# Gate rows of the expert layer: one wide comparison on VectorE, three gated rows on GpSimd, two plain rows on ScalarE

## The reference, cut to what matters

```python
s1 = jnp.einsum('thd,kd->thk', q[..., :half], sub_keys[0])
s2 = jnp.einsum('thd,kd->thk', q[..., half:], sub_keys[1])
v1, i1 = lax.top_k(s1, PEER_TOPK)
v2, i2 = lax.top_k(s2, PEER_TOPK)
top, pos = lax.top_k(cand, PEER_TOPK)      # cand: v1 + v2, all 16 x 16 pairs
eidx = jnp.take_along_axis(cidx, pos, axis=-1)   # i1 * 128 + i2
gate = jax.nn.softmax(top, axis=-1)
act = jax.nn.gelu(jnp.einsum('td,thkd->thk', hc, expert_u[ec]))
return jnp.einsum('thk,thkd->td', gate * act, expert_v[ec])
```

## Time and profile before

| | |
|---|---|
| median of 3 runs | 3121.25 us (3119.77 to 3121.68) |
| the profiled execution | 3119.68 us, its span 3117.9 us |
| TensorE busy | 2938.2 us (94%) |
| VectorE busy | 1988.4 us (64%) |
| ScalarE busy | 1313.5 us (42%) |
| GpSimd busy | 270.8 us (9%) |
| mean granted TensorE clock | 0.97 |

### The profile page before, as it was taken

How to read it: one execution, slowest core, us unless ns; L and a number is a source line. 1 busy time by engine, 2 the same in 40 slices (tenths; PEclk the granted TensorE clock), 3 DMA queues, 4 the chain that set the end, 5 groups by cost and what they waited for, 6 DMA issues and landing times.

```text
span 3117.9 us, 48959 instructions
## 1 busy us (share of the span) xinstructions
PE 2938.2 (94%) x17330; PEld 2555.8 (82%) x17330; DVE 1988.4 (64%) x3635; ACT 1313.5 (42%) x2096; POOL 270.8 (9%) x387
## 2 busy tenths in 40 slices
PE   8897899999999987988999999998999898999898
PEld 5674799999999864877999999997977887978797
DVE  4669866777767634797666666665556654555664
ACT  1235844444444412575444444444443433534333
POOL 0026600000000000473000000000000000000000
PEclk9898999999999997999999999999999998999899
DMA  8532166666666641303555665664334454424354
GB/s 329 193 114 81 42 189 222 226 232 229 223 233 231 204 156 71 143 8 108 189 187 186 195 191 191 194 193 164 128 132 166 152 186 150 151 108 163 141 176 148
DMA packets 130807, 524.30 MB, mean 168 GB/s; under 512 B 17981, under 2 KB 28093, under 8 KB 108025
## 3 DMA queue, kind: packets, MB, share of 16 engines
q1 hardware_dynamic: 120648, 508.13, 47.6%
q10 hardware_dynamic: 10034, 14.52, 1.4%
HBM read 519.44 MB, written 3.16 MB: 168 GB/s over the span
## 4 chain that ended last, share of the span: by engine, by line
PE 76%; issue 8%; DVE 6%; ACT 6%; DMA 1%; DVEq 1%; ACTq 1%; PEld 0%; POOL 0%; SPq 0%; PEldq 0%; POOLq 0%
PE prob_ps L1247 22%; PE acc L1259 22%; PE acc L927 7%; PE acc L912 3%; PE acc L1474 3%; PE acc L886 3%; PE acc L1489 3%; PE acc L865 3%; PE acc L1424 2%; ACT arena L1810 2%; PE turn_ps L1020 2%; PE acc L1449 1%; PE acc L994 1%; ACT arena L1800 1%; PE turn_ps L940 1%
## 5 line engine op out<-in xcount | busy, mean ns | idle before, releaser
L1247 PEld LDWEIGHTS prob_ps<-hTr,utr 128*128 128x128 f32 x5856 | 734.5, 191 | 26.5 <-issue 8.6
L1247 PE MATMUL prob_ps<-hTr,utr 128*128 128x256 f32 x5856 | 745.4, 284 | 2.3 <-issue 1.2
L1259 PE MATMUL acc<-vr,wtr 128*128 128x512 f32 x2964 | 718.8, 391 | 1.1 <-DVE vr L2550 1.1
L1259 PEld LDWEIGHTS acc<-vr,wtr 128*128 128x128 f32 x2964 | 541.0, 188 | 103.9 <-issue 1.7
L2550 DVE TENSOR_TENSOR vr<-slab,vr 128x1024 fp32r<-128x1024 f32 x246 | 301.4, 1225 | 408.3 <-ACT vr L1848 408.3
L1848 ACT CAST vr<-slab 128x1024 fp32r<-128x1024 f32 x246 | 258.2, 1050 | 577.8 <-PE acc L1259 570.0
L2525 DVE TENSOR_TENSOR utr<-slab,utr 128x1024 fp32r<-128x1024 f32 x244 | 297.3, 1218 | 11.9 <-ACT utr L1821 11.9
L1821 ACT CAST utr<-slab 128x1024 fp32r<-128x1024 f32 x244 | 255.4, 1047 | 8.2 <-issue 4.8
L2104 POOL TENSOR_TENSOR small<-small 128x2 f32<-128x2 f32 (+3 forms) x18 | 20.8, 1155 | 2695.5 <-DVE small L2176 1458.0
L2807 DVE TENSOR_TENSOR slab_lo<-slab,w_hi 128x2048 fp32r<-128x2048 f32 x64 | 143.8, 2288 | 124.1 <-ACT w_hi L2076 124.1
L2076 ACT CAST w_hi<-slab 128x2048 fp32r<-128x2048 f32 x64 | 119.2, 1906 | 159.2 <-DMA slab<-in_pack_b 150.7
(11 more groups left out here) (292 smaller groups left out, 4137.6 us busy)
## 6 DMA issues: line engine op xcount, KB each, us to landing
slab<-in_pack_b SPq DMA_DIRECT2D x132, 1024.0 KB, 4.9
slab<-in_peer_v SPq DMA_DIRECT2D x255, 512.0 KB, 3.5
slab<-in_peer_u SPq DMA_DIRECT2D x244, 512.0 KB, 4.6
arena<-in_pack_a SPq DMA_DIRECT2D x84, 512.0 KB, 4.7
slab<-in_pack_a SPq DMA_DIRECT2D x40, 1024.0 KB, 7.1
arena<-in_peer_u SPq DMA_DIRECT2D x6, 1024.0 KB, 14.2
slab<-in_pack_b SPq DMA_DIRECT2D x4, 832.0 KB, 5.4
arena<-in_pack_a SPq DMA_DIRECT2D x2, 1024.0 KB, 18.6
```

Source lines behind the costliest of these rows:

```text
L1247: ins = pe.matmul(prob_ps[:, m % 2, 0:S], utr[:, m % 2, uh, k * P:k * P + P], hTr[:, hh, k, :], start=(k == 0 and n == 0), stop=(k == KD - ...
L1259: ins = pe.matmul(y_ps[:, t, n, :], wtr[:, m % 2, wh, t * P:t * P + P], v[:, vh, n * 512:n * 512 + 512], start=first and k == 0, stop=last ...
```

## The change

GpSimd makes the first three gated rows (POOLQ = 3) in place of four plain ones; a gated row compares and multiplies in one instruction and reads two values for each partition. ScalarE makes the first two plain rows (ACTQ = 2) in place of three in the middle. VectorE makes the other six plain rows by one instruction, a comparison of two tiles (128 x 768, `iota` repeated over the rows against the keys repeated along the columns), and then the five gated rows 3 to 7. The number of instructions in a group goes from 9 to 6 on VectorE, from 4 to 3 on GpSimd and from 5 to 4 on ScalarE, counting its copy. GpSimd additionally waits at the start of a layer for the copy of the gates, "pairs1", and two semaphores get other names.

```diff
-POOLQ = 4
+POOLQ = 3
-ACTQ = 3
+ACTQ = 2
...
-                    at = n * TOKG + POOLQ
+                    at = n * TOKG
                     for q in range(ACTQ):
                         act.activation(key_gap[:, q], iota[:], ACT.Square, bias=pairsT[:, 1, at + q:at + q + 1], scale=-1.0)
                     act.drain()
-                    act.activation(rows[:, n % 2, 1, POOLQ:POOLQ + ACTQ, :], key_gap, ACT.Relu, bias=1.0, scale=-1.0)\
+                    act.activation(rows[:, n % 2, 1, 0:ACTQ, :], key_gap, ACT.Relu, bias=1.0, scale=-1.0)\
                         .then_inc(act_rows.sem, 1)
...
-                nc.gpsimd.wait_ge(*turns.emptied_at("a", l, "pairs0"))
-                nc.gpsimd.sem_inc(passed["pool"], 1)
+                for use in ("pairs0", "pairs1"):
+                    nc.gpsimd.wait_ge(*turns.emptied_at("a", l, use))
+                    nc.gpsimd.sem_inc(passed["pool"], 1)
                 for n in range(S // TOKG):
...
-                        ins = nc.gpsimd.tensor_scalar(rows[:, n % 2, 1, q, :], iota[:], pairsT[:, 1, tok:tok + 1],
-                                                      None, ALU.is_equal)
-                    ins.then_inc(plain_rows.sem, 1)
+                        ins = nc.gpsimd.tensor_scalar(rows[:, n % 2, 0, q, :], iota[:], pairsT[:, 0, tok:tok + 1],
+                                                      pairsT[:, 2, tok:tok + 1], ALU.is_equal, ALU.mult)
+                    ins.then_inc(pool_rows.sem, 1)
...
                 for n in range(S // TOKG):
                     dve.wait_ge(*gates_full.two_before("a", l, n + 1))
-                    for q in range(TOKG):
+                    at = n * TOKG + ACTQ
+                    dve.tensor_tensor(rows[:, n % 2, 1, ACTQ:TOKG, :], spread(iota[:], 1, TOKG - ACTQ),
+                                      spread(pairsT[:, 1, at:at + TOKG - ACTQ], 2, P), ALU.is_equal)
+                    for q in range(POOLQ, TOKG):
                         tok = n * TOKG + q
-                        dve.tensor_scalar(rows[:, n % 2, 0, q, :], iota[:], pairsT[:, 0, tok:tok + 1],
-                                          pairsT[:, 2, tok:tok + 1], ALU.is_equal, ALU.mult)
-                    for q in range(POOLQ + ACTQ, TOKG):
-                        tok = n * TOKG + q
-                        ins = dve.tensor_scalar(rows[:, n % 2, 1, q, :], iota[:], pairsT[:, 1, tok:tok + 1], None,
-                                                ALU.is_equal)
-                    ins.then_inc(gated_rows.sem, 1)
+                        ins = dve.tensor_scalar(rows[:, n % 2, 0, q, :], iota[:], pairsT[:, 0, tok:tok + 1],
+                                                pairsT[:, 2, tok:tok + 1], ALU.is_equal, ALU.mult)
+                    ins.then_inc(dve_rows.sem, 1)
```

More of the change, by code:

```diff
@@ L286, in two_blocks @@
         pairs_ready = Signal(sem("pairs_ready"), a=2)
-        gated_rows = Signal(sem("gated_rows"), a=S // TOKG)
-        plain_rows = Signal(sem("plain_rows"), a=S // TOKG)
+        dve_rows = Signal(sem("dve_rows"), a=S // TOKG)
+        pool_rows = Signal(sem("pool_rows"), a=S // TOKG)
         act_rows = Signal(sem("act_rows"), a=S // TOKG)
@@ L1225, in _ @@
                 for n in range(S // TOKG):
-                    pe.wait_ge(*gated_rows.at("a", l, n + 1))
-                    pe.wait_ge(*plain_rows.at("a", l, n + 1))
+                    pe.wait_ge(*dve_rows.at("a", l, n + 1))
+                    pe.wait_ge(*pool_rows.at("a", l, n + 1))
                     pe.wait_ge(*act_rows.at("a", l, n + 1))
```

## The result

The changed kernel takes 3171.93 us (median of 4 runs, 3166.99 to 3174.36) against 3121.47 (4 runs). The ratio is 1.016, with a 95% interval of 1.0142 to 1.0178: slower by 1.6%, some 50 us. The forecast was 3124.2 with a range of 3110 to 3142, so the result lies 30 us above its upper end. The profiled execution took 3171.95, its span 3170.2.

What follows compares the result with a forecast made beforehand. ScalarE's chain was taken to bound the gates stage at 2.561 us a group; afterwards a loop of 2.60: 59 x (2.60 - 2.561) = +2.3, start +0.6, together +2.9 us, median 3124.2 us, range 3110 to 3142.

Steps and rivals of the forecast that it cites:

- ScalarE's load: Gates stage, kernel before: ScalarE's chain sets the period of 2.561 us a group; after the change its load is 2.17.
- the stage's time is carried to the end one to one: Expert loop behind the gates stage: TensorE busy 523.85 of 524 us, so the stage's gain or loss isn't hidden there.
- VectorE's wide comparison: Gates stage, VectorE: the 768-column two-tile instruction takes 0.97 us, bounds 0.9 and 1.74; VectorE's load becomes 2.34 us.
- ScalarE's relu of 256 columns: Gates stage, ScalarE: relu covers 256 columns instead of 384, which took 0.52 us; 128 columns are worth about 0.10.
- GpSimd's hold: Gates stage: VectorE's wide comparison holds a GpSimd row by up to 0.84 us in each group, 64 times.
- TensorE is released by GpSimd: Sign expected in the trace after: TensorE's groups wait for GpSimd's rows, with the copies 2.60 us apart.
- The second rival: GpSimd's multiply costs a pass: decides from a 0.72 row; 0.80 gives +13 us, 0.98 gives +29, 3150; chance 0.28.
- GpSimd's row at 0.68: Gates stage: an undisturbed gated row on GpSimd takes 0.68 us, between 0.59 and 0.98; three are 2.04.
- The second value: GpSimd's gated row: reading a second value per partition adds about 0.065 us, as much as the first.
- a second operation may ride along: GpSimd's gated row: from below the multiply costs nothing, each column already taking 2.5 ns; from above 0.32 us.
- 1.58 + 1.5 x row: Gates stage: period from a two-group loop through VectorE, hold, GpSimd's three rows and TensorE; 2.60 us at row 0.68.

Runs made afterwards that it cites:

- The run without the gate: Changed kernel, but GpSimd's three rows leave out the multiply with the gate and the second value per partition: 0.9988 of the kernel before, 3118.38 us.
- the one with TensorE kept busy: Changed kernel, but TensorE makes two matmuls more in each group before waiting for the rows: ratio 1.0116 to the kernel before, 3153.68 us.
- the old split with the gated row: Kernel before, but GpSimd's four plain rows are also multiplied with the gate, no wide comparison: ratio 1.0168 to the kernel before, 3170.96 us.
- the constant: Changed kernel, but GpSimd multiplies with the constant 1.0 instead of the token's gate: ratio 1.0075 to the kernel before, 3140.9 us.

## Why the prediction was wrong

**Right.** The bound before was ScalarE's load and the stage's time is carried to the end one to one (46.7 us of difference in the two stages; from the last copy to the program's end the two kernels differ by 2.4). VectorE's wide comparison takes 0.958 us (forecast 0.97). ScalarE's relu of 256 columns takes 0.416 (0.42). GpSimd's hold exists, is caused by the second SBUF input, and is 0.65 to 0.8 us in a group. TensorE is released by GpSimd. The second rival named the mechanism that decided, the multiply, and its threshold, a row of 0.72, was passed; but it was priced by the same formula as the forecast, at 3150 at most.

**The step that failed first: GpSimd's row at 0.68.** The second value was put at 0.065 and is 0.073. The multiply was put at next to nothing, on the ground that "a second operation may ride along", and it costs 0.113; another 0.04 to 0.08 come on top beside VectorE's rows (not tested by itself), so that a row takes 0.82 on average. The range of 0.59 to 0.98 held it. Without a row for the operation, the middle of the two bounds (0.78) would have been nearer than the lower quarter. Three rows at 0.14 more are 0.42 us.

**The second: the hold was put in a loop and not in the load.** I let the hold overlap with the time in which GpSimd waits for TensorE, and got 1.58 + 1.5 x row. But a full engine doesn't wait: the hold stands in its load, 3 x row + 0.66. At a row of 0.68 this gives 2.70 and not 2.60; at 0.82 it gives 3.12, where my formula gives 2.81. The run without the gate (2.37 by the load, 2.47 by the loop, 2.38 measured) and the one with TensorE kept busy (3.14, 2.81, 3.11) both side with the load. I had a row for each load and never wrote the sum for GpSimd, 3 x 0.68 + 0.84, which is 2.88 and above all other loads. Neither step alone would have left the range: by the forecast's own sum a row of 0.82 in the loop gives 3137 (59 x 0.25 more than before) and the load at 0.68 gives 3130 (59 x 0.14); both together, 3.12 us a group, give 3155.

**What was not in the forecast: the clock.** TensorE idled for 1.85 to 1.98 us before each pair of groups, the granted clock fell to 0.50 for 3.4 us five times in a layer, a group then took 3.4 us of matmuls, and this went into the group's time: 0.20 of 3.31.

Together: 3.12 for the load, 0.20 for the clock, 3.32 against 3.31 measured; less 2.55 and times 62 that is 48 us, against 46.7.

**The rest of the 52.3 us of the spans.** The first copy comes 2.2 us earlier, the matmuls of the second layer's early experts (line 1219) take 46.9 us from the first start to the last in place of 42.4, and the second block 2.4 longer, as in the other kernels here, where it is 1.3 to 4.5 longer (about 1 us is scattered). The 4.5 is in untouched code, in which VectorE and GpSimd share out the choice of the picks by instructions with two SBUF inputs. TensorE works on beside them, turns the picks (line 940) and then makes the last 16 of these matmuls. Before and after:

```profile
1347.51 0.60 PE L940 MATMUL turn_ps<-ident,arena 128*128 128x128 f32 x4
...
1348.70 3.62 PE L1219 MATMUL prob_ps<-hT,arena 128*128 128x256 f32 x16
```

```profile
1371.96 0.66 PE L940 MATMUL turn_ps<-ident,arena 128*128 128x128 f32 x4 [2.25 <-DVE arena L1541]
...
1373.59 5.04 PE L1219 MATMUL prob_ps<-hT,arena 128*128 128x256 f32 x16
```

In the changed kernel TensorE idled 2.25 us for VectorE, and then the granted clock fell to 0.50 for 3.4 us (from 1373.0), which made the 16 matmuls 1.4 us longer. Part of VectorE's delay is that its instructions stood behind GpSimd's. The same eight instructions of VectorE (count | busy us, mean ns | idle before) in the kernel before and in the changed one:

```profile
L1525 DVE TENSOR_TENSOR arena<-arena,small 128x512 f32<-128x512 f32 x8 | 5.2, 693 | 0.3
```

```profile
L1525 DVE TENSOR_TENSOR arena<-arena,small 128x512 f32<-128x512 f32 x8 | 7.3, 953 | 0.3
```

GpSimd came some 0.6 us earlier to its part, measured from the first of the matmuls of line 1219, and the two engines' instructions fell into another order (eight others of VectorE, line 1533, took 0.7 us less). In the profiled executions the kernel before and the old split with the gated row have 42 us here, and all eight kernels with the new split have 47, faster ones too: in these ten traces it goes with the split. Why GpSimd came earlier wasn't tried.

What stays open is why the two layers fall into different steps with the constant, and hence how long such a step lasts: no run was made that sets the start.

## What to carry to other kernels

Write down the load of each engine that is moved work, with everything that another engine's instruction takes from it, before looking at loops: the largest load is a floor under the period. GpSimd's price for 128 columns depends on the form: 0.60 us for a comparison with a value per partition, 0.71 with a multiply by a constant, 0.78 with a multiply by a second value, each undisturbed; so give it the plainest form. When VectorE must run a wide instruction with two tiles beside GpSimd, let one of the tiles lie in PSUM if it is there anyway.

## What the hardware showed that I had not expected

- A wide comparison with its second tile in PSUM costs VectorE nothing (0.954 against 0.958 us) and frees GpSimd of a hold of 0.65 to 0.8 us. The Trainium skill (SBUF — State Buffer, "Who interferes with whom") says that it is the second SBUF input of such an instruction that contends with GpSimd's reads; the runs agree, with one such input and with two.
- Two more matmuls in a group made the kernel faster by 0.4%, because the clock stayed up.
- TensorE busy for 61% of a stage, in even pauses of 1.24 us, kept clock 1.00; the changed kernel, with about as long a group but its groups in pairs, had 0.90; the constant's slow layer, also in pairs, had 1.00. What decides isn't shown.
- The same code ran at 2.57 and at 2.93 us a group in two layers; what differed was when GpSimd's rows began against VectorE's wide comparison.
- In the steady parts a GpSimd row that began up to 0.20 us before VectorE's wide comparison was held, and one that began 0.21 us or more before it was not.
